# The FFN up-projection as seven block products, and the down-projection as a phase of its own

## The reference, cut to what matters

```python
m = gate[:, :, 0] * (o_a @ w_proj_a) + gate[:, :, 1] * (o_b @ w_proj_b)
x = x + m @ w_o
h = rmsnorm(x, norm2_g)
u = h @ w_up                       # (rows, 1024) @ (1024, 5632)
c = conv_b + conv_w[0]*u[t-2] + conv_w[1]*u[t-1] + conv_w[2]*u[t]   # per channel
a, b = split(c, 2)                 # 2816 channels each
x = x + (gelu(a) * b) @ w_down     # (rows, 2816) @ (2816, 1024)
y = rmsnorm(x, norm_f_g)
```

## Time and profile before

| what | value |
|---|---|
| median of three runs | 1989.45 us |
| span of the profiled execution (first to last instruction) | 1980.4 us |
| median less span | 9.05 us |
| PE busy | 1861.0 us, 94% of the span |
| PEld busy | 1595.6 us, 81% |
| DVE busy | 998.5 us, 50% |
| ACT busy | 588.2 us, 30% |
| POOL busy | 117.6 us, 6% |
| mean rate of all DMAs | 138 GB/s |

### The profile page before, as it was taken

How to read it: one execution, slowest core, us unless ns; L and a number is a source line. 1 busy time by engine, 2 the same in 40 slices (tenths; PEclk the granted TensorE clock), 3 DMA queues, 4 the chain that set the end, 5 groups by cost and what they waited for, 6 DMA issues and landing times. The chain is left out here.

```text
span 1980.4 us, 30755 instructions
## 1 busy us (share of the span) xinstructions
PE 1861.0 (94%) x11646; PEld 1595.6 (81%) x11646; DVE 998.5 (50%) x1993; ACT 588.2 (30%) x984; POOL 117.6 (6%) x209
## 2 busy tenths in 40 slices
PE   7999999999778887899989999999999999999996
PEld 5777778999645555666678889999999999999995
DVE  5202443000264796666666365546545555555657
ACT  4212001111584585333432133122122213212213
POOL 0000000000100301323200001000000000000000
PEclk9999999999988889999989999999999999999998
DMA  6444446611622928999947115112102102102102
GB/s 224 173 172 172 172 172 247 247 46 46 171 45 66 328 87 294 386 385 392 348 166 258 36 43 177 37 33 64 33 30 64 42 21 64 42 21 64 43 16 109
DMA packets 138165, 274.27 MB, mean 138 GB/s; under 512 B 23097, under 2 KB 75978, under 8 KB 135690
## 3 DMA queue, kind: packets, MB, share of 16 engines
q1 hardware_dynamic: 116170, 154.46, 23.4%
q0 software_dynamic: 21888, 118.38, 16.3%
HBM read 243.24 MB, written 78.97 MB: 163 GB/s over the span
## 5 line engine op out<-in xcount | busy, mean ns | idle before, releaser
L2191 DVE TENSOR_TENSOR tl_x<-tl_x,tl_ps 128x512 f32<-128x512 f32 (+1 forms) x198 | 135.3, 687 | 186.9 <-PE tl_ps L2419 183.9
L498 PE MATMUL tl_ps<-tl_T_lo,tl_up_hi 128*128 128x364 f32 (+1 forms) x1008 | 222.2, 329 | 0.0
L498 PE MATMUL tl_ps<-tl_T_hi,tl_up_lo 128*128 128x364 f32 (+1 forms) x1008 | 222.2, 329 | 0.0
L498 PE MATMUL tl_ps<-tl_T_hi,tl_up_hi 128*128 128x364 f32 (+1 forms) x1008 | 222.2, 329 | 0.0
L498 PEld LDWEIGHTS tl_ps<-tl_T_hi,tl_up_hi 128*128 128x128 f32 x1008 | 174.9, 188 | 0.9
L498 PEld LDWEIGHTS tl_ps<-tl_T_hi,tl_up_lo 128*128 128x128 f32 x1008 | 174.8, 188 | 0.0
L498 PEld LDWEIGHTS tl_ps<-tl_T_lo,tl_up_hi 128*128 128x128 f32 x1008 | 174.8, 188 | 0.0
L468 PE MATMUL fr_ps<-fr_w_hi,h_hi 128*128 128x512 f32 x384 | 154.1, 401 | 2.4 <-DVE h_lo L364 2.4
L468 PE MATMUL fr_ps<-fr_w_lo,h_hi 128*128 128x512 f32 x384 | 152.5, 397 | 0.0
L468 PE MATMUL fr_ps<-fr_w_hi,h_lo 128*128 128x512 f32 x384 | 152.5, 397 | 0.0
L2419 PE MATMUL tl_ps<-tl_dn_hi,tl_f_hi 128*128 128x512 f32 x360 | 141.0, 392 | 0.0
(11 more groups left out here) (332 smaller groups left out, 3409.6 us busy)
## 6 DMA issues: line engine op xcount, KB each, us to landing
out_s<-in_cache POOLq DMA_DIRECT2D x8, 4080.0 KB, 20.3
all_lead<-in_w_up SPq DMA_DIRECT2D x44, 512.0 KB, 4.8
fr_raw<-in_w_in POOLq DMA_DIRECT2D x9, 2048.0 KB, 8.8
pg_pages<-in_pool POOLq DMA_DIRECT2D x64, 256.0 KB, 6.5
pg_pages<-in_pool SPq DMA_DIRECT2D x64, 256.0 KB, 7.2
pg_odds<-in_pool SPq DMA_DIRECT2D x64, 256.0 KB, 8.1
zs<-fr_zt SPq DMA_DIRECT2D x48, 256.0 KB, 2.0
tl_dn_raw<-in_w_down SPq DMA_DIRECT2D x22, 512.0 KB, 4.5
```

Source lines behind the costliest of these rows:

```text
L498: last = pe.matmul(out[:, n * 512:n * 512 + b - a], lhs, rhs[:, a:b], start=(i == 0), stop=(i == len(pairs) - 1))
L2191: dve.tensor_tensor(x, x, banks[m % len(banks)][0:n, :], ALU.add).then_inc(added, 1)
```

## The change

The first three channel tiles (`PLAIN_UP`) are made as before, except that ACT copies each product out of PSUM (`evict`) to `u0` or `u1` and the convolution reads it there. The other 19 (`UNITS`) are made by seven block products each: the weights of a tile are 2 x 2 blocks (two halves of `D_MODEL` by gate and value half), the rows 2 x 2 blocks (two halves of `D_MODEL` by two sides of 544 rows, `SIDE`). Each product is 4 chunks x 3 passes x 2 matmuls of 272 columns.

The sums of row blocks (`T1` to `T4`) are made once by DVE; the sums of weight blocks (`S1` to `S4`) by POOL, in place in the loaded weights, four per unit. The products add up in PSUM; ACT keeps three partial results and DVE finishes the four blocks of `u` in SBUF. POOL stores each tile of `f` to the DRAM scratch `fd`, and the residual to `x2d`.

The down product then runs alone: three groups of three row tiles, each 22 steps. A step loads one tile of `w_down` (512 KB) and 384 rows of `f` (192 KB), splits both on ACT and DVE, and issues 18 matmuls of 512 columns (16 in the third group). Six banks of a group accumulate over its 22 steps, and DVE adds each to `x2` once. The rows lie with 32 sample rows at either end, so that both sides have 544.

```diff
+            def multiply(s_, name, bank, hi, lo, first):
+                pe.wait_ge(lo_made, block_no(name, s_) + 1)
+                w_hi, w_lo = (slots[:, SLOT_OF[name], part, :, :] for part in range(2))
+                for k in range(KH):
+                    for m, (w, h) in enumerate(three_passes(w_hi, w_lo, hi, lo)):
+                        for n in range(2):
+                            last = pe.matmul(ps[:, (bank + n) * 512:(bank + n) * 512 + SIDE // 2], w[:, k, :],
+                                             h[:, k, n * SIDE // 2:(n + 1) * SIDE // 2], start=(first and k == 0 and m == 0),
+                                             stop=(k == KH - 1 and m == 2), skip_group_check=True)
+                last.then_inc(p_ready, 1)
...
-            with pe.Fori(1, PAIRS - 1) as i:
-                up(i * 2, 0)
-                down(i - 1)
-                up(i * 2 + 1, 1)
...
+            p1(0)          # and p2, p6, p5, p7 of unit 0
+            for s_ in range(UNITS):
+                if s_ + 1 < UNITS:
+                    p1(s_ + 1)
+                p4(s_)
+                p3(s_)
+                if s_ + 1 < UNITS:
+                    p2(s_ + 1)
+                    p6(s_ + 1)
+                    p5(s_ + 1)
+                    p7(s_ + 1)
+            for n in range(STEPS):
+                down(n)
```

```diff
+            def sum_s2(s_):                                   # POOL
+                pool.wait_ge(lo_made, block_no("S3", s_) + 1)
+                x = weights(s_, "S2")
+                pool.tensor_tensor(x, x, weights(s_, "A22"), ALU.add).then_inc(sum_made, 1)
...
+            for s_ in range(UNITS):                           # POOL
+                if s_ + 1 < UNITS:
+                    sum_s2(s_ + 1)
+                    sum_s1(s_ + 1)
+                    sum_s4(s_ + 1)
+                if s_ + 2 < UNITS:
+                    sum_s3(s_ + 2)
+                store(PLAIN_UP + s_)
...
+            for s_ in range(UNITS):                           # ACT, cut to more = True
+                    head(s_ + 1, "A12")
+                    head(s_ + 1, "S3")
+                    keep_p1(s_ + 1)
+                    head(s_ + 1, "S2")
+                    head(s_ + 1, "S1")
+                finish_c21(s_)
+                last_tap(j, 1)
+                    head(s_ + 1, "A22")
+                    head(s_ + 1, "S4")
+                last_tap(j, 0)
+                    head(s_ + 2, "A11")
+                    keep_u2(s_ + 1)
+                gelu(j)
+                    keep_u3(s_ + 1)
...
+            for s_ in range(UNITS):                           # DVE, cut to more = True
+                finish_c22(s_)
+                    rest(s_ + 1, "A12")                       # and S3, S2, S1
+                convolve(j, 1)
+                finish_c12(s_)
+                    rest(s_ + 1, "A22")
+                    finish_c11(s_ + 1)
+                convolve(j, 0)
+                    rest(s_ + 1, "S4")
+                    rest(s_ + 2, "A11")
+                product(j)
...
+            def load_step(n):                                 # SP
+                g, k = divmod(n, FT)
+                if n < 2:
+                    sp.wait_ge(lo_made, 7 * UNITS)
+                else:
+                    sp.wait_ge(dn_lo_done, n - 1)
+                    sp.wait_ge(f_lo_done, n - 1)
+                sp.dma_start(dn_raw[:, n % 2, :], a["w_down"][k * P:k * P + P, :]).then_inc(dn_in[n % 2], 16)
+                if g == 0:
+                    sp.wait_ge(f_stored, 16 * (k + 1))
...
+                    sp.dma_start(f_raw[:, n % 2, :], fd[k, :, c0:c0 + 3 * P]).then_inc(f_in[n % 2], 16)
...
+            for n in range(STEPS):                            # SP
+                if n == 4:
+                    sp.wait_ge(p_ready, made("P3", UNITS - 1))
+                    sp.dma_start(x2[:, 0:QT, :], x2d[0:SEQ, :].rearrange("(t p) d -> p t d", p=P)).then_inc(x2_back, 16)
+                    sp.dma_start(x2[0:SROWS, QT, :], x2d[SEQ:ROWS, :]).then_inc(x2_back, 16)
+                load_step(n)
```

More of the change, by code:

```diff
@@ L1834, in tail_stage @@
[L1834 to L1837, removed]
@@ L1848, in _, with turned_bank, f_count @@
+        def turned_bank(t, u):
+            got = tp[:, u * D:(u + 1) * D].rearrange("p (k r) -> p k r", k=KD)[:, :, 0:rows_of(t)]
+            return got.rearrange("p k (s r) -> p k s r", s=2) if t == QT else got
+        def f_count(n):
+            return 16 * sum(1 if m < 2 * FT else 2 for m in range(n % 2, n + 1, 2))
         @block.sync
@@ L1911, in _ @@
[L1911 to L1921, removed]
+            load_up(0, up_raw, up_in)
@@ L1922, in _ @@
+            for i in range(6, RT):
+                store(i)
             for i in range(YS):
@@ L2061, in _ @@
[L2061 to L2076 removed]
+            evict(0, 0)
@@ new lines, in _ @@
+            last_tap(0, 0)
+            head_sum(0)
+            evict(0, 1)
+            last_tap(0, 1)
+            gelu(0)
+            head_up(2)
+            head_sum(1)
+            evict(1, 0)
+            last_tap(1, 0)
+            head_sum(2)
+            evict(1, 1)
+            last_tap(1, 1)
+            gelu(1)
+            head(0, "A11")
+            head(0, "A12")
+            head(0, "S3")
+            head(0, "S2")
+            evict(2, 0)
+            last_tap(2, 0)
+            evict(2, 1)
@@ L2078, in _ @@
+            for n in range(4, STEPS):
+                step_heads(n)
+                if n >= FT and 2 <= n % FT < 5:
+                    final_square(NORMS[n // FT - 1][0] + n % FT - 2)
+                if n >= FT and n % FT == 6:
+                    final_root(n // FT - 1)
+            for g in (2, 3):
+                for i in range(*NORMS[g]):
+                    final_square(i)
+                final_root(g)
         @block.vector
@@ new lines, in _ @@
+            convolve(0, 0)
+            less_rest(t_tmp[:, :, :], B11_lo, 5)
+            rest_sum(0)
+            convolve(0, 1)
+            product(0)
+            rest_up(2)
+            rest_sum(1)
+            dve.wait_ge(t_lo_done, 1)
+            dve.wait_ge(t_step, 5)
+            less(t_two, t_two, B21_hi)
+            convolve(1, 0)
+            less_rest(t_two, B21_lo, 6)
+            rest_sum(2)
+            convolve(1, 1)
+            product(1)
+            rest(0, "A11")
+            rest(0, "A12")
@@ L2343, in _ @@
+            for m in range(12, 18):
+                add_out(m)
+                if m == 17:
+                    finish(2)
+            finish(3)
         @block.tensor
```

844 lines of the change are left out of this document (493 added, 351 removed).

## The result

The changed kernel takes 1937.5 us, the median of four runs (1934.9 to 1940.3), against 1989.6 for the kernel before: a ratio of 0.974, 95% interval 0.973 to 0.976. Two further sets on other occasions gave 1939.3 (0.9744, 0.972 to 0.977) and 1938.7 (0.9743, 0.973 to 0.976). The forecast of 1951 had the sign and the mechanism; the gain was 52 us where it said 38.5, and 1937.5 lies just outside its range of 1940 to 1995.

A forecast was written before the change was run, and what follows sets the result against it. PE's pace was taken as the bound: 1245.87 + 415.4 + 259.4 + 1.9 + 1.1 + 3.0 + 1.5 = 1928.2, + 13.7 = 1941.9, 38.5 under 1980.4; so 1989.45 - 38.5 = 1951 us, range 1940 to 1995 (8 in 10).

The forecast's parts named there:

- 3192 block matmuls: Up product of the 19 changed tiles: 3192 matmuls of 272 columns at 130.1 ns, 415.4 us, 40.5 less.
- seams of the units: PE waits where units begin and end: first `p1` for the last eviction 1.9 us, last unit's `keep_u3` 1.1.
- down phase with its stalls: Down product: 1144 matmuls of 512 columns, 259.4 us, plus 3.0 for one transfer and 1.5 for collisions.
- last matmul to end of span: Last adds, norms and store after the last matmul: 13.7 us, 2.1 less than before (0 to 4).
- span to median of the runs: Profiled span of the kernel before lies 9.05 us under its runs' median; carried over to the forecast time.
- The line through both: Matmul pace by width, through 363 columns (166.6 ns) and 512 (226.75 ns): 0.403 ns per column, 130.1 at 272.
- the layout of the unit: Engine order in a 21.9 us unit: PE waits for nothing while a GpSimd sum costs under about 2.8 us.
- rival B: Feed of the down phase sets the pace: at 4.6 us a step, 34 us more, 1985; chance 0.11.
- The reload of `x2`: Down phase: 4.25 MB of `x2` in front of step 4's load makes PE wait 3.0 us (0 to 6).
- C: In the units, GpSimd sums over 2.8 us make PE wait at p5 and p7; at 4.2, 2001; chance 0.10.
- D: Up product: weight load sets a floor for short matmuls; at 150 ns 63 us more, 2014; chance 0.08.
- E: Seams, row sums or first units stall PE by 15 to 25 us in all; 1971; chance 0.11.

The follow-up runs named there:

- The second experiment: Changed kernel plus, behind its down phase, 60 matmuls at each of eight widths, then 60 with another weight tile each: 125.5 ns at 272 columns.
- experiment 6: Changed kernel with the reload of `x2` in nine pieces, not one: 1934.1 us beside 1939.3, and 1933.0 beside 1938.7.
- experiment 9: Changed kernel with more GpSimd adds before each sum: one more, 1962.7 us (0.987 of the kernel before); two more (second kernel), 2071.5 (1.041).
- experiment 4: Changed kernel with all 22 tiles by plain products, no units or sums, down phase of its own kept: 2004.7 us, 1.0072 of the kernel before.

## Why the prediction was right, and where it was wrong

The bound was read rightly, and so was the place of the gain: PE's list of matmuls sets the stage before and after. By its own terms, against the profiled execution of the changed kernel:

| term | forecast, us | measured, us | difference |
|---|---|---|---|
| start of the plain half tiles | 1185.9 | 1191.3 | +5.4 |
| 3192 block matmuls | 415.4 | 401.0 | -14.4 |
| seams of the units | 3.0 | 1.9 | -1.1 |
| down phase with its stalls | 263.9 | 268.6 | +4.7 |
| last matmul to end of span | 13.7 | 13.0 | -0.7 |
| span to median of the runs | 9.05 | 1.7 | -7.4 |

The differences sum to -13.5, which is the whole miss. From the start of the stretch to the end of the span they sum to -11.5: 50.0 us less where 38.5 had been forecast.

**The step that failed: "The line through both has 0.403 ns per column; at 272 columns it gives 130.1 ns."** The mechanism was right and the size off: 125.5 ns. The two points had 15 and 13 ns over their streaming; a line through them turns that difference of 2 ns into a slope and carries it further down, to 17 over the streaming. With the columns' own slope (1 / 2.4 = 0.417 ns) and 13 to 15 ns on top the same rows give 126 to 128. 4.6 ns times 3192 is the 14 us. The second experiment is what shows it: 125.5 ns at 272 columns outside the units too. The same error set the lower end of the range, which took 127 ns for the fastest pace. (By its own terms, 3.1 x 3192 ns and the 3.0 of the stall less than 1951, that end is 1938 and not 1940.)

**The other one: "The span lies 9.05 under the median of the runs shown."** It was taken over into the result as if it lay around every span. For the changed kernel time and span differ by 1.67 us (1937.47 against 1935.8), for the kernel before in its second profile by 1.7. The rest was the short execution: 5.9 us in stages ahead of the stretch. Against a usual execution of the kernel before (span 1986.3) the changed one's 1935.8 is 50.5 less. The two parts came back with opposite signs as the first and last row of the table; together they are 2 us of the miss, and the pace is the rest.

**What held.** The plain tiles took 60.01. The up product waits for nothing in a unit, and the layout of the unit was right: `finish_c12` was put 9.7 + 2 x 1.28 = 12.3 us after p7's end and came 12.5 after it. GpSimd's sum was bounded at 0.65 and 2.28 and measured 1.28 and 1.74. The Trainium skill's estimate from the page GPSIMD Engine Reference, section Performance versus the Vector engine, had been 1.1 us and some start-up, 1.7 at most with the ports shared. The trace agrees with the first, 1.28; the second, for which no working is given, came out a little low, with 1.74 in the mean. (That the ports are shared stands in the same page's section Specifications.) The down steps run at PE's pace (324 matmuls in 75.22 us, 1.6 of it lost to the lower clock at their start), so rival B is refuted: the load of `w_down` lands in 3.7 us here (median), under the 5.0 that it has. The tail was 13.0. The last matmul ended at 1922.75, far from the 1950 that would have made the forecast fail.

**Smaller misses.** The reload of `x2` gave one stall, at the step where it was put, but of 4.7 us instead of 3.0 (0 to 6), 6.1 in another profile, and 1.6 more behind it at the lower clock, which the forecast didn't have at all: 6.3 in all, most of the down phase's + 4.7. That the edit of experiment 6 won 5.2 and 5.7 us, more than the 3.5 us of wait at this step that it took away, agrees with it. The seams of the units were shorter: 1.2 and 0.7 us of wait. And the chances don't add up: C and D alone are 0.18, where "slower" was given 0.16.

**The rivals.** C is refuted for this kernel and shown as a mechanism; its place was right, its limit 2.6 a sum instead of 2.8, and its price far too low. The forecast put the gain's end at 3.9 us a sum. With 1.04 to 1.38 us an instruction, the second kernel of experiment 9 had S2 and S1 in 7.5 us (1389.33 to 1396.78), 3.7 each, and was already 4% slower than the kernel before. D is refuted at 272 columns and would have been right at 192, where the line gives 98 ns and the run shows 112. E is refuted by the list of waits.

**What stays open.** Why the overhead of a matmul is 12.1 ns at 272 columns and 16.0 at 448 isn't settled, nor why a unit behind a wait of 1.05 us takes 21.4 us at clock 1.00 and not 21.1. Nor is what makes the clock differ from one execution to another between 500 and 700 us.

## What to carry to other kernels

Where one engine's list bounds a stage, fewer columns pay even in more and shorter instructions, as long as the width stays over the floor: count instructions at the pace of their own form, as streaming plus a constant, and don't carry a slope through two points far beyond them: 2 ns between the points became 5 at the end of the line. Make the sum from the start of the stretch that changes, and take what lies ahead of it and around the span from more than one execution. A wait of some 5 us on PE costs more than its length, because the clock falls with it, and moving work to GpSimd frees DVE of much less than the work: here 8 of 27 us.

## What the runs showed of the hardware

- A 128x512 float32 add on GpSimd took 1.28 us beside an idle DVE and 1.74 beside a busy one; DVE's instructions on two SBUF tensors went from 0.687 to 0.871 (128x512) and from 1.284 to 1.515 (128x1023) in the mean. With two more adds on GpSimd before each sum the smallest form grew most: 128x64 from 0.279 to 0.723.
- float32r matmuls with 128 rows of weights: pace is the streaming plus 12 to 16 ns from 256 to 512 columns, with a weight load in front of each, of a new tile or of the same one again; at 192 columns some 112 ns.
- After 5.1 us without a matmul the granted clock was 0.50 for the next 4 us, after 4.7 us likewise at first (0.50 over 1675 to 1677), after the 4.0 us in experiment 4 it was 0.58 over the next 4 us. After the waits of 1.05 us in experiment 9 a unit's 168 matmuls took 21.4 us, hardly more than 21.1.
